# Four-layer streaming encoder: DeltaNet levels one unit later, inversions spread over six units, VectorE splitting the RG-LRU weights, recurrence loads and modulation loads moved ahead

## The reference

```python
mod = silu(c) @ ada_w[layer] + ada_b[layer]          # shift, scale, gate of a layer
# RG-LRU: u = causal_dwconv(u, conv_w) + conv_b; r, i = sigmoid(u @ gate_w + gate_b)
#         hs = linear_scan(a, mult * i * u);  y = hs * silu(gate);  y @ w_out
# gated DeltaNet, in chunks, 8 heads of 128:
q, k, v = split(silu(causal_dwconv(h @ w_in, conv_w)))
A = where(strict, (k * beta) @ k.T * decay, 0)       # T = I + A, solved against v and k
v_new = u_c - w_c @ state
o = (q * exp(g)) @ state + attn_intra @ v_new
state = state * exp(g_last) + k_dec.T @ v_new
y = rms_norm(o, norm_w) * silu(z);  y @ w_out
```

## Time and profile before

| | |
|---|---|
| median of 3 runs | 3631.87 us (3631.03 to 3632.08) |
| profiled execution | 3634.57 us, span 3632.8 us |
| PE busy | 3328.7 us (92% of the span) |
| PEld busy | 2687.6 us (74%) |
| DVE busy | 2364.5 us (65%) |
| ACT busy | 1467.0 us (40%) |
| POOL busy | 1019.0 us (28%) |
| mean granted TensorE clock | 0.953 of full |

### The profile page before, as it was taken

The page is one execution under the profiler, slowest core; times in us unless marked ns, Lnnn a source line. Parts: engine busy times, 40 slices in busy tenths (PEclk is TensorE's granted clock), DMA queues, the critical chain, the costliest instruction groups (busy, mean ns, idle before and its releaser), DMA issues.

```text
span 3632.8 us, 49174 instructions
## 1 busy us (share of the span) xinstructions
PE 3328.7 (92%) x18887; PEld 2687.6 (74%) x18887; DVE 2364.5 (65%) x3858; ACT 1467.0 (40%) x2561; POOL 1019.0 (28%) x517
## 2 busy tenths in 40 slices
PE   4997889799889999999969998998998999999997
PEld 3676668678787777888747776776878777788876
DVE  6897878964456774555567766787645554555554
ACT  3664355433344113322436654653334431342232
POOL 1123323311133224222411242432111422422242
PEclk6998899899999999999989999998999999999999
DMA  4333545454652532111231122544549211221112
GB/s 167 95 111 119 152 114 148 120 134 134 228 190 85 159 105 81 54 36 36 70 122 49 51 59 63 164 132 126 139 114 341 70 59 53 64 71 36 36 53 87
DMA packets 569014, 383.82 MB, mean 106 GB/s; under 512 B 67802, under 2 KB 522445, under 8 KB 568781
## 3 DMA queue, kind: packets, MB, share of 16 engines
q1 hardware_dynamic: 568781, 380.68, 34.7%
HBM read 299.01 MB, written 80.54 MB: 104 GB/s over the span
## 4 chain that ended last, share of the span: by engine, by line
PE 76%; DVE 15%; issue 3%; ACT 2%; DMA 2%; POOL 1%; SPq 1%; ACTq 0%; DVEq 0%; POOLq 0%
PE bank L229 59%; DVE dnp_conv L1733 2%; DVE res_ada_sums L278 2%; DVE h_lo L681 1%; PE bank L2222 1%; PE bank L2425 1%; DVE res_sq_total L705 1%; DVE dnp_diag_term L1811 1%; DVE res_h L669 1%; PE bank L2452 1%; PE bank L2011 1%; PE bank L1994 1%; PE bank L2466 1%; DVE dnp_diag_inv L1814 1%; PE bank L1425 1%
## 5 line engine op out<-in xcount | busy, mean ns | idle before, releaser
L229 PE MATMUL bank<-h_hi,w_hi 128*128 128x512 f32 x3616 | 1475.8, 408 | 61.4 <-POOL w_lo L211 19.6
L229 PE MATMUL bank<-h_lo,w_hi 128*128 128x512 f32 x3616 | 1426.7, 395 | 0.0
L229 PE MATMUL bank<-h_hi,w_lo 128*128 128x512 f32 x3616 | 1426.2, 394 | 0.0
L211 POOL TENSOR_TENSOR w_lo<-w_raw,w_hi 128x1024 fp32r<-128x1024 f32 x292 | 727.6, 2493 | 1765.8 <-ACT w_hi L203 1765.8
L229 PEld LDWEIGHTS bank<-h_hi,w_hi 128*128 128x128 f32 x3616 | 690.7, 191 | 240.6 <-issue 68.4
L229 PEld LDWEIGHTS bank<-h_lo,w_hi 128*128 128x128 f32 x3616 | 691.2, 191 | 148.3 <-issue 13.0
L229 PEld LDWEIGHTS bank<-h_hi,w_lo 128*128 128x128 f32 x3616 | 689.5, 191 | 150.0
L1733 DVE SCALAR_TENSOR_TENSOR dnp_conv<-dnp_raw,dn_conv_w,dnp_conv 128x512 f32<-128x512 f32 x288 | 255.8, 888 | 139.2 <-ACT dnp_conv L1555 131.8
L203 ACT ACTIVATE w_hi<-w_raw 128x1024 fp32r<-128x1024 f32 x292 | 305.8, 1048 | 78.7 <-DMA w_raw<-in_rg_w_out 22.7
L721 DVE SCALAR_TENSOR_TENSOR x_res<-bank,mod_gate,x_res 128x512 f32<-128x512 f32 x128 | 96.0, 750 | 271.5 <-PE bank L229 270.4
L781 ACT ACTIVATE res_sq<-x_res 128x512 f32<-128x512 f32 x160 | 100.9, 631 | 366.7 <-DVE x_res L721 320.9
(11 more groups left out here) (312 smaller groups left out, 4426.2 us busy)
## 6 DMA issues: line engine op xcount, KB each, us to landing
dnr_in<-dn_planes SPq DMA_DIRECT2D x112, 512.0 KB, 7.6
dn_planes<-y SPq DMA_DIRECT2D x192, 256.0 KB, 2.5
w_raw<-in_dn_w_in SPq DMA_DIRECT2D x64, 512.0 KB, 4.4
w_raw<-in_swa_w_in SPq DMA_DIRECT2D x36, 512.0 KB, 3.6
w_raw<-in_rg_w_in SPq DMA_DIRECT2D x32, 512.0 KB, 4.1
w_raw<-in_rg_w_out SPq DMA_DIRECT2D x32, 512.0 KB, 4.0
w_raw<-in_dn_w_out SPq DMA_DIRECT2D x32, 512.0 KB, 4.0
w_raw<-in_pool_w_in SPq DMA_DIRECT2D x32, 512.0 KB, 4.1
```

The costliest lines, as they stand in the source:

```text
L211: self.nc.gpsimd.tensor_tensor(self.lo[j % SLOTS][:, :, :], self.raw[j % 2][:, :, :], self.hi[j % SLOTS][:, :, :].bitcast(F32), ALU.subtra ...
L229: ins = self.nc.tensor.matmul(out, w[slot][:, k, :], x[:, k, cols], start=(k == 0 and n == 0), stop=(k == KT - 1 and n == 2))
```

## The change

It has nine edits. The ingest loads the modulation pieces before the weights, gives them two accumulators, adds eight of them inside the second 512 columns, and lets ACT take x out of PSUM in both halves; SP stores the attention's bias table from there too. `rg_phase` adds four pieces a unit (`per` is now 48 divided by 12), reads the sums at the last unit, and has DVE make `w_lo`. In `dn_project_phase` the transposes of alpha and beta come after product 2 and `k_rows(0)` after product 3; both batches of the inversion have twelve parts over six units; the store of the first batch and the first loads of inverses go to the first unit of part two; `level_first(u)` stands behind the second product of unit u, and `level_second(u)` and the copies are in unit u + 1. The recurrence's first seven loads are issued ahead of the fence, the last stores of the projections are handed over to its SP, and its last block does AT before the update of the state. The final phase copies to its stage with DVE and ACT, one half each. The diff, cut to its core:

```diff
@@ ingest and residual phase
-            ada = Modulation(core, ctx, A, [(0, SHIFT), (0, SCALE)], tag, core.bank[3], D, 0, 1, places)
+            ada = Modulation(core, ctx, A, [(0, SHIFT), (0, SCALE)], tag, core.bank[3], D, 0, 2, places)
             if ada:
+                ada.load(sp, 0, ada.pieces)
                 w.load_to(sp, tile0 + 2)
-                ada.load(sp, 0, ada.pieces)
...
             for j, (c, d) in enumerate(steps):
-                if ingest:
-                    ins = nc.vector.tensor_copy(here, ring[j % 2][:, :])
+                if ada and c > 0:
+                    ada.accumulate(dve, d, d + 1)
             if ada:
-                ada.accumulate(dve, 0, ada.pieces)
+                ada.accumulate(dve, KT, ada.pieces)
...
+                if ingest:
+                    act.wait_ge(*projected(j))
+                    nc.scalar.activation(x[:, d, cs[c]], ring[j % 2][:, :], ACT.Copy).then_inc(s_x, 1)
...
+            if final:
+                for t in range(HALF // P):
+                    act.wait_ge(s_tout, 2 * t + 2)
+                    if t >= 2:
+                        act.wait_ge(s_out[t % 2], 16 * (t // 2))
+                    nc.scalar.activation(stage[t % 2][:, CH:D], core.bank[3][:, :], ACT.Copy).then_inc(s_stage[1], 1)
@@ rg_phase
-            per = -(-ada.pieces // units)
+            per = -(-ada.pieces // (units - 4))
-            for n in range(KT):
-                w.subtract_to(pool, tile0 + 2 * n + 4)
             for i in range(units):
                 convolve(i)
+                if ada and i == units - 1:
+                    ada.finish(dve)
+                w.subtract_to(dve, tile0 + 2 * (i // NCH) + 3 + i % NCH, V)
@@ dn_project_phase, SP
-                if u == 15:
-                    store_diag(0)
-                if u == UNITS - 1:
-                    for ahead in range(LB):
-                        load_inverses(ahead)
                 if u == 0:
                     keep_k(UNITS - 1)
+                    store_diag(0)
                     keep_a(UNITS - 1)
-                    load_grams(1)
-                    load_grams(2)
+                    load_inverses(0)
-                if u == 5:
+                if u == 7:
                     store_diag(1)
-                if u and u + 2 < UNITS:
-                    load_inverses(u + 2)
-                    load_grams(u + 2)
+                if u + 1 < UNITS:
+                    load_inverses(u + 1)
+                    load_grams(u + 1)
@@ dn_project_phase, PE
                 project(2 * u, u // 2 * 2)
-                if u:
+                if u == 1:
+                    turn_ab(0)
+                    turn_ab(1)
+                elif u:
                     k_rows(u - 1)
...
                 project(2 * u + 1, u // 2 * 2 + 1)
                 if u == 0:
-                    turn_ab(0)
-                    turn_ab(1)
                 if u == 1:
+                    k_rows(0)
...
                 project(32 + 2 * u, UNITS + u // 2 * 2)
                 if u == 0:
                     k_rows(UNITS - 1)
-                level_first(u)
-                if u:
+                else:
+                    level_second(u - 1)
                     v_rows(u - 1)
                 project(32 + 2 * u + 1, UNITS + u // 2 * 2 + 1)
                 if u == 0:
                     gram(UNITS - 1)
-                level_second(u)
+                level_first(u)
@@ dn_project_phase, DVE
-                if 10 <= u < 15:
-                    invert(0, 2 * (u - 10), 10)
+                if u >= 10:
+                    invert(0, 2 * (u - 10), 12)
...
-                if 1 <= u < 5:
-                    invert(1, 2 * (u - 1), 8)
+                if 1 <= u < 7:
+                    invert(1, 2 * (u - 1), 12)
-                level(u)
+                if u:
+                    level(u - 1)
@@ dn_recur_phase
+            load_first(KQ)
+            load_first(QE)
+            store_inverse(sp, UNITS - 2)
+            load_first(VR)
+            store_last_v(sp)
+            load_first(KD)
+            load_first(YT)
+            load_first(AT)
+            store_inverse(sp, UNITS - 1)
+            load_first(ZS)
+            all_stored(sp)
-            core.fence(pe)
+            core.fence(pe, ENGINES[:4])
+                if b < NB - 1:
+                    update_state()
+                loaded(AT, b)
...
+                if b == NB - 1:
+                    update_state()
```

180 lines of the change are left out of this document (106 added, 74 removed).

## The result

The changed kernel takes 3599.91 us (median of 4 runs, 3597.65 to 3602.15), against 3631.97 us of the kernel before on the same chip. The ratio is 0.9915 [0.99, 0.993]: 32 us less, about half of the 64.5 us that the sum promised, and ten us above the range.

A forecast was written before the change was run, and what follows sets the result against it. It took TensorE as the bound (busy 3328.7 of 3632.8 us), with only idle time and half clock to win. Terms summed to 64.5 us off the profiled 3634.57, giving 3570.1, less 2.7 for the median: forecast 3567, range 3545 to 3590.

The forecast's parts named there:

- A: Ingest: the norm comes 8 us sooner in the first half, and 1.8 us are won in the second half's ingest.
- C: Start of the projections: waits for transposes and w_lo shrink, 10.7 us won in the first half and 10.4 in the second.
- G: Last block of the recurrence: the wait at L1983 shrinks, 2 us won a half.
- B: Recurrent layer: the wait at its end shrinks, 17.9 us won in the first half and 0.8 in the second.
- H: Final stages: copies split between DVE and ACT, 4 us won in the first half and 3 in the second.
- 3: Recurrent layer: DVE bounds it at 13.2 to 13.8 us a unit, 9 to 17 us lost, 3576 to 3584; chance 0.07.
- 4: Part two of the projections: every level step waits, in all 16 units, giving 3651 us; chance 0.04.
- 5: Early recurrence loads or modulation do nothing: 10.6 or 8 us less gain, 3576; chance 0.07.
- Rival 1: Inversion and levels cost more: units 1 to 6 of part two wait 3 us each, clock falls, 3585; chance 0.18.
- E: Level steps one unit later in part two: PE waits for DVE's copies in units 1 to 6, 6 us lost a half.
- D: First level step of part two: PE still waits 11.6 us, but 2.5 and 2.8 us are won in the two halves.
- F: Early recurrence loads: the recurrence's first matmul starts 5.3 us sooner in each half.

The follow-up runs named there:

- e10: The kernel of e8 with the recurrence's first seven loads put back behind all stores and the fence: 3555.28 us, ratio 0.98.
- e2: Changed kernel with SP's first inverse store and loads ahead of keep_k(15) and keep_a(15), and store_diag(1) at the head of unit 7: 3581.16 us, ratio 0.9867.
- e1: Changed kernel with DVE's level copies ahead of its part of the inversion in units 1 to 6 of part two: 3576.59 us, ratio 0.9855.
- e5: Changed kernel with D and E undone (level steps, inversions and SP's stores and loads around them as before): 3579.68 us, ratio 0.9866.
- e3: Changed kernel with SP's wait for all stores moved behind the loads of recurrence block 1: 3593.23 us, ratio 0.99.
- e8: Changed kernel with the edits of e1, e2 and e3, and w_lo of units 11, 13 and 15 of part one moved to DVE: 3538.14 us, ratio 0.9762.
- e9: The kernel of e8 with the w_lo of part two also made by DVE: 3574.94 us, ratio 0.9853.
- e6: The kernel before with the recurrent layer's edits alone (fourth piece a unit, w_lo by DVE, sums read at the last): 3615.24 us, ratio 0.9958.
- e7: Changed kernel with the recurrent layer's w_lo back on POOL: 3598.44 us, ratio 0.9917.

## Why the prediction came out too low

**Right in place and size.** A (9.3 for 8), C (21.2 for 21.1) and G (4.5 for 4). C's total is closer than its parts: PE's waits there shrank by 18.3 us where 19.4 were put, and the clock gave the other 2.9 where 1.7 were put. B's first half, 17.0 for 17.9, went by the row of the second half's gap and found exactly that gap (5.27, where 4.5 was put); `w_lo` on DVE took 1225 ns where 1.23 us was put (the row it was put by has 1.285), and it made the long forms of the stretched line vanish (750 to 753 ns for all 96, where the earlier trace rows had up to 2781). H's first half, 4.4 for 4. The side was right as well (faster, 0.94). Of the rivals, 3 is refuted (units still 12.65 us on PE, DVE at 162 of 188 us), 4 did not happen, and 5 is refuted by A's 9.3 us for the modulation and by e10 for the loads. Rival 1, "the inversion and the levels cost more", is true by its title and beyond its price, but not by its mechanism: it had PE wait 3 us for DVE in each of units 1 to 6, and only two of the six came near that.

**E, the step that failed: "Summed over six units: 1.7, 0, 1, 0.75, 2.8, 0.1, say 6".** The mechanism was named rightly for the waits on DVE: level copies behind the inversion part, stretched by POOL's `w_lo`. The size was 32.6 us for 12, for two reasons.
- The waits for DVE are 6.6 us a half (2.81, 0.86 and 2.90 in units 1, 4 and 5), so the prediction's sum of 6 held. It was the clock that was left out of the term: behind each wait of over 2 us a product takes 7.1 to 7.8 instead of 5.7 us. The prediction priced that at 1.5 us and then put it beside the sum, as what it would be if two waits a half reached 3 us. They reached 2.8 and 2.9, and both paid it (1.6 each in the first half, 1.6 and 2.1 in the second).
- A third long wait was not in it at all, 2.31 us at 825.11 (2.25 in the second half) for `dnp_decay_upper`, in unit 8, past the place from which "DVE is ready at 5.1, two us early"; neither were three short ones for loads behind it (0.80; 1.28 and 0.96). DVE was ready; the load was not, because it is issued behind `store_diag(1)` and the inverse loads on SP. The prediction looked at DVE alone in these units, and a load queue that is a unit closer to its use was a part of the same edit. e2 takes it away by moving the store.

e1 shows the first reason (22 us, of which 13.1 of wait and about 4 x 1.6 of clock are accounted for), e2 the second with D's, e5 that the whole of D and E costs 28 us where it stands.

**D: "PE got there at 724.3 ... and waits 11.6".** It waited 11.48, the best hit of the list, and the gain came out at 3.0 for 5.3; in the second half it waited 9.53, behind 4.57 us for DVE's `y` just before. What the prediction did not ask is what the same row offered: the inverses are ready 5.5 us before their store leaves, and e2 takes 14.5 of the 21 us back by order on SP alone.

**F: 5.3 us.** The first matmul came 4.9 and 5.3 us sooner, as forecast, though the end of the last product is 945.95 in the trace and not "near 946.65". The step that failed is the next one: what is late next. The term ended at the first matmul and put nothing for the steps behind it. There the load of YT came 2.33 us late in the first half, and block 1's loads stayed behind the wait for all stores, which the early start had not moved; 1.9 and 2.7 us were gone by block 1. e3's edit gets 2.5 us a half of it back by the marks; in its time alone it can't be told from the noise.

**B's second half, "0.8".** The gap in front of the restart is 5.27 us before and after, so nothing came of the 0.8. The -1.65 stands in front of it, and not from the change. In the second half, at the start of the layer, the window of the changed kernel is

```profile
1893.33:1918.33 25.00, 25.00 (x96) 18.85 (x97) 17.04 (x26) 15.18 (x20) 0.00 (x0) 0.93 0.24 73
```

while e2, whose code is the same there, has

```profile
1888.07:1913.07 25.00, 25.00 (x103) 19.35 (x104) 18.23 (x29) 15.18 (x20) 0.00 (x0) 1.00 0.24 74
```

The wait ahead is 2.94 us in the one and 2.95 in the other. The layer lasts 1.6 us longer where the clock fell.

**What stays open.** The pooling layer moves by more than most terms between profiles of kernels with the same code there: 312.3 us in the changed kernel and e1, 316.7 before, 317.1 in e2, 321.6 in e5. In e5 DVE's adds of the modulation meet a `w_lo` of POOL at their start (4.64 us for three) and PE waits 3.4 us; in the changed kernel the three take 3.13 and the wait is 1.45. No run was made to hold that meeting fixed, so 4.4 us of the changed kernel's gain and the 7 us missing in e5's profile are only put down to it. Why H brings 1.5 for 3 in the second half was not looked into.

## What to carry to other kernels

Moving a step one unit later buys time only if its inputs, on every queue, come no later than it: write down for DVE and for the DMA queue alike what stands ahead of them, and put short copies that PE waits for ahead of long work that nobody waits for. Price each new wait of PE at its length plus the half clock that may follow it (1.4 to 2.1 us here behind each of 2.3 to 2.9 in front of a level step), and count that in the sum, not beside it. Before an instruction goes to a less loaded engine, ask what buffer it frees and who is queued for it: the same edit gave 12 us in e8 and took 33 in e9.

## What the runs showed of the hardware that was not expected

- The granted clock is not a function of the wait. Behind 2.94 and 2.95 us at the same place it was 0.93 and 1.00 over 25 us (above). Ten profiles (all but e6 and e7) have a wait of 2.94 to 2.96 us there, and the product behind it takes 6.0 us in five of them and 6.3 to 7.7 in the other five. In the kernel before, 1.58 us left it at 1.00; in e9 a wait of 1.91 us was enough to lose it:

```profile
774.93:777.93 3.00, 3.00 (x29) 2.49 (x30) 1.82 (x5) 1.89 (x4) 0.00 (x0) 0.70 1.02 297
```

  The Trainium skill, TensorE: Matmul & The Clock Gate, What's actually happening, says that the chip watches activity on a rhythm of its own, not bound to the kernel, so that the point of the switch varies between runs. The two runs above agree with that; they don't prove it.
- A 128x1024 `w_lo` takes DVE 1225 ns and POOL 2494 on the mean, and POOL's also lengthens one instruction of DVE by about 2.03 us. Moving it to DVE made DVE less busy, not more (162.1 against 173.2 us in e7).
